# A two-block transformer kernel: the order of the first projection's columns, adaptive-weight units beside value turning, squares at the front of the sparse heads

## The reference

```python
mod = silu(c) @ w_ada + b_ada                       # six chunks: shift, scale, gate, twice
h = rms_norm(x, g_attn_pre) * (1 + scale_a) + shift_a
d_q, d_k, d_v, s_q, s_k, s_v, i_q, i_k, i_w = split(h @ w_in)      # 5456 columns
# differential attention, 8 heads: rope on q1,q2,k1,k2; (softmax(q1 k1) - lam * softmax(q2 k2)) v; rms_norm of the output
# sparse attention, 8 heads: score[t,s] = sum over 16 index heads of i_w[t,h] * relu(i_q[t,h] . i_k[s]);
#   each query keeps its 64 best keys; softmax over those; one key and one value for all heads
mixed = concat(diff_out, dsa_out) @ w_o
```

## Time and profile before

| | |
|---|---|
| three runs | 2812.94 us (median; 2812.19 to 2818.18) |
| the profiled execution | 2820.23 us, span 2818.4 us |
| mean granted TensorE clock | 0.945 of full speed |
| PE busy, share of the span | 92% |
| DVE, ACT, POOL busy | 51%, 37%, 10% |
| DMA queues | 503.83 MB, mean 179 GB/s |

### The profile page before, as it was taken

The page is one execution under the profiler, slowest core; times in us unless marked ns, Lnnn a source line. Parts: engine busy times, 40 slices in busy tenths (PEclk is TensorE's granted clock), DMA queues, the critical chain, the costliest instruction groups (busy, mean ns, idle before and its releaser), DMA issues. The chain is left out here.

```text
span 2818.4 us, 47985 instructions
## 1 busy us (share of the span) xinstructions
PE 2606.4 (92%) x19936; PEld 2404.8 (85%) x19936; DVE 1433.0 (51%) x1866; ACT 1040.0 (37%) x1322; POOL 284.3 (10%) x369
## 2 busy tenths in 40 slices
PE   5999988969999999999789979799899999999998
PEld 3888846949999999999779937358799999999998
DVE  3577756856764444344353354524455555554443
ACT  3523244334333343333243325223344444443332
POOL 4000121420000000011221000101100000000000
PEclk8999989979999999999889979779899999999999
DMA  8777866936775555555535402003455555554553
GB/s 300 260 278 271 258 215 236 330 110 237 259 272 184 181 191 179 170 188 181 156 106 170 151 15 75 15 1 120 141 172 180 181 186 181 179 179 165 179 190 108
DMA packets 263852, 503.83 MB, mean 179 GB/s; under 512 B 17168, under 2 KB 26299, under 8 KB 263483
## 3 DMA queue, kind: packets, MB, share of 16 engines
q1 hardware_dynamic: 249888, 492.99, 52.2%
q10 hardware_dynamic: 13867, 9.50, 1.3%
HBM read 498.05 MB, written 2.10 MB: 177 GB/s over the span
## 5 line engine op out<-in xcount | busy, mean ns | idle before, releaser
L1220 DVE TENSOR_TENSOR w_lo<-raw,w_hi 128x2048 fp32r<-128x2048 f32 (+2 forms) x386 | 862.1, 2233 | 1019.9 <-ACT w_hi L776 1019.3
L1788 PE MATMUL bank<-x_hi,w_hi 128*128 128x256 f32 (+3 forms) x4608 | 1314.1, 285 | 51.6 <-DVE w_lo L1220 18.8
L1789 PE MATMUL bank<-x_lo,w_hi 128*128 128x256 f32 (+3 forms) x4608 | 1311.0, 284 | 0.0
L1790 PE MATMUL bank<-x_hi,w_lo 128*128 128x256 f32 (+3 forms) x4608 | 1309.0, 284 | 0.0
L776 ACT ACTIVATE w_hi<-raw 128x2048 fp32r<-128x2048 f32 (+2 forms) x386 | 719.4, 1864 | 1070.2 <-PE bank L1790 919.1
L1788 PEld LDWEIGHTS bank<-x_hi,w_hi 128*128 128x128 f32 (+1 forms) x4608 | 876.9, 190 | 77.7 <-DVE w_lo L1220 38.6
L1790 PEld LDWEIGHTS bank<-x_hi,w_lo 128*128 128x128 f32 (+1 forms) x4608 | 877.9, 191 | 0.0
L1789 PEld LDWEIGHTS bank<-x_lo,w_hi 128*128 128x128 f32 (+1 forms) x4608 | 873.7, 190 | 0.2 <-issue 0.2
L1788 PE MATMUL bank<-hid_hi,w_hi 128*128 128x256 f32 x1408 | 400.6, 285 | 7.9 <-POOL hid_lo L662 6.6
L1789 PE MATMUL bank<-hid_lo,w_hi 128*128 128x256 f32 x1408 | 399.9, 284 | 0.0
L1790 PE MATMUL bank<-hid_hi,w_lo 128*128 128x256 f32 x1408 | 399.8, 284 | 0.0
(11 more groups left out here) (279 smaller groups left out, 1545.3 us busy)
## 6 DMA issues: line engine op xcount, KB each, us to landing
raw<-in_w_ada SPq DMA_DIRECT2D x88, 1024.0 KB, 6.0
raw<-in_w_gate SPq DMA_DIRECT2D x88, 1024.0 KB, 5.2
raw<-in_w_up SPq DMA_DIRECT2D x88, 1024.0 KB, 5.2
raw<-in_w_in SPq DMA_DIRECT2D x68, 1024.0 KB, 5.7
raw<-in_w_down SPq DMA_DIRECT2D x64, 1024.0 KB, 5.0
raw<-in_w_down SPq DMA_DIRECT2D x32, 768.0 KB, 4.3
raw<-in_w_o SPq DMA_DIRECT2D x16, 1024.0 KB, 6.9
raw<-in_w_out SPq DMA_DIRECT2D x16, 1024.0 KB, 5.1
```

What stands on the lines that cost most here:

```text
L1220: dve.tensor_tensor(w_lo[ps][:, 0:width], raw[slot][:, 0:width], w_hi[ps][:, 0:width], ALU.subtract).then_inc(raw_free[slot], 1)
L1788: pe.matmul(out, wh[:, k, c], hi(k0 + k), start=a0, stop=False)
L1789: pe.matmul(out, wh[:, k, c], lo(k0 + k), start=False, stop=False)
L1790: ins = pe.matmul(out, wl_[:, k, c], hi(k0 + k), start=False, stop=z)
```

## The change

Four things.

1. The projection's columns come in another order: differential queries and keys before sparse queries. Rotation 2 is now that of the differential queries, 3 that of the differential keys, 4 that of the sparse queries; gathers, scatters and POOL's wait counts follow.
2. The four units of w_ada block `ADA_INDEX` stand between the value turnings, those of the next block beside index heads 4 to 7. The last rotation (r = 4) stands after index head 5 on PE and after index head 6 on DVE.
3. ACT puts all eight pieces of rotation 3 back before the ReLU of index head 0, and the four of rotation 4 after index heads 8 to 11. PE waits for the return of rotations 2 and 3 before head 0, and for that of rotation 4 before head 8; ACT waits for it at g = 3, before it overwrites the gathering tile.
4. ACT's squares for the differential heads stand at the front of each step of the sparse heads.

```diff
-ORDER_IN1 = [10, 8, 9, 6, 7, 0, 1, 2, 3, 4, 5]
+ORDER_IN1 = [10, 8, 9, 0, 1, 2, 3, 6, 7, 4, 5]
...
-            (rows_iq[:, :, :], 0, RA), (rows_sq[:, :, :], 2, RB), (rows_d[:, 0:2, :], 0, RA), (rows_d[:, 2:4, :], 0, RA))]
+            (rows_iq[:, :, :], 0, RA), (rows_d[:, 0:2, :], 0, RA), (rows_d[:, 2:4, :], 0, RA), (rows_sq[:, :, :], 2, RB))]
...
                 elif n == 6:
-                    gather(2, 32, T_SQ, rows_sq)
+                    gather(2, 16, T_DQ, rows_d[:, 0:2, :])
...
                 elif n == 8:
-                    gather(3, 16, T_DQ, rows_d[:, 0:2, :])
+                    gather(3, 16, T_DK, rows_d[:, 2:4, :])
...
                 elif n == 10:
-                    scatter(2, 32, T_SQ, rows_sq)
-                    gather(4, 16, T_DK, rows_d[:, 2:4, :])
+                    scatter(2, 16, T_DQ, rows_d[:, 0:2, :])
+                    gather(4, 32, T_SQ, rows_sq)
...
+            scatter(3, 16, T_DK, rows_d[:, 2:4, :])
+            take_row(ADA_INDEX)
             for h in range(16):
...
-                if h in (3, 11):
-                    take_row(ADA_INDEX + h // 8)
-                elif h in (7, 15):
+                if h in (3, 12):
                     take_columns(ADA_INDEX + h // 8)
-                if h < 8:
-                    scatter(3, 16, T_DQ, rows_d[:, 0:2, :], h)
-                else:
-                    scatter(4, 16, T_DK, rows_d[:, 2:4, :], h - 8)
+                elif h == 8:
+                    take_row(ADA_INDEX + 1)
+                if 8 <= h < 12:
+                    scatter(4, 32, T_SQ, rows_sq, h - 8)
...
                 for g in range(g0, g1):
+                    if kind(g) == "dsa":
+                        act.wait_ge(h_taken, g - 7)
+                        squares("diff", part=g - 8)
...
+                        if g == 3:
+                            act.wait_ge(rows_back[4], 16 * 4)
                         take_out(g - 1)
-                    if kind(g) == "dsa":
-                        act.wait_ge(h_taken, g - 7)
-                        squares("diff", part=g - 8)
...
+            ada_quarter(ADA_INDEX, 0)
             pe.wait_ge(bank_freed, BLOCKS_IN1 * 4 + 4)
-            turn_values(0, [proj[:, T_DV + h, :] for h in range(8)] + [proj[:, T_SV, :]], False)
-            rotate_rows(4)
+            turn_values(0, [proj[:, T_DV + h, :] for h in range(8)] + [proj[:, T_SV, :]], False,
+                        lambda j: ada_quarter(ADA_INDEX, j // 3 + 1) if j % 3 == 1 else None)
...
-                if h % 8 < 4:
-                    ada_quarter(ADA_INDEX + h // 8, h % 8)
-                elif h % 8 == 7:
-                    ada_columns(ADA_INDEX + h // 8)
+                if h == 2:
+                    ada_columns(ADA_INDEX)
+                elif 4 <= h < 8:
+                    ada_quarter(ADA_INDEX + 1, h - 4)
+                elif h == 10:
+                    ada_columns(ADA_INDEX + 1)
+                if h == 5:
+                    rotate_rows(4)
...
+                if g == 8:
+                    pe.wait_ge(rows_back[4], 16 * 4)
...
-            pe.wait_ge(rows_back[2], 16 * 4)
-            for r in (3, 4):
+            for r in (2, 3):
                 pe.wait_ge(rows_back[r], 16 * 8)
```

More of the change, by code:

```diff
@@ L706, in _ @@
             for r, (src, sin, cos, _, _, _) in enumerate(turns1):
-                pool.wait_ge(rows_in[r], 16 * (2, 8, 4, 8, 8)[r])
+                pool.wait_ge(rows_in[r], 16 * (2, 8, 8, 8, 4)[r])
                 if r >= 2:
@@ L1451, in _ @@
             take_values(0, 9, 2, lambda j: vtok[:, :, j, :])
-            add_rows(4)
             dve.wait_ge(iw_turned, 1)
@@ L1469, in _ @@
                 ins.then_inc(i_added, 1)
+                if h == 6:
+                    add_rows(4)
             dve.wait_ge(i_added, 16)
@@ L1977, in rotate, with turn_values @@
                     ins.then_inc(r_sum, 1)
-            def turn_values(first, tiles, meta):
+            def turn_values(first, tiles, meta, beside=None):
                 for j, src in enumerate(tiles):
@@ L1989, in turn_values @@
                     ins.then_inc(v_turned, 1)
+                    if beside is not None:
+                        beside(j)
+            ada_quarter(ADA_INDEX, 0)
             pe.wait_ge(bank_freed, BLOCKS_IN1 * 4 + 4)
-            turn_values(0, [proj[:, T_DV + h, :] for h in range(8)] + [proj[:, T_SV, :]], False)
-            rotate_rows(4)
+            turn_values(0, [proj[:, T_DV + h, :] for h in range(8)] + [proj[:, T_SV, :]], False,
+                        lambda j: ada_quarter(ADA_INDEX, j // 3 + 1) if j % 3 == 1 else None)
             pe.wait_ge(r_out, 4)
```

## The result

The changed kernel takes 2802.44 us (median of 20 runs, 2795.9 to 2815.53). The kernel before takes 2816.95 us in the same comparison (20 runs, 2806.73 to 2832.08). The ratio is 0.9947, with a 95% interval of 0.9933 to 0.9961: about 14.9 us faster, between 11 and 19, where 18.7 were forecast.

What follows compares the result with a forecast made beforehand. PE, 92% busy, bounds the kernel; gains come where it idles or runs at low clock. 17.0 + 1.7 - 0 = 18.7 us off gives 2794.2 us (from a 2812.94 median); range 2788 to 2806, forecast's own 2790 to 2799.

Steps and rivals of the forecast that it cites:

- The return of the rows: Ahead of head 0: differential rows, last issued at about 351.7, are back at 358.5, 11 us early; the 7.33 us wait goes.
- The start of the index heads: Behind the value turnings: index head 0 can start near 351.6 (before 352.22), the first ReLU near 352.4 (before 353.90).
- Four units ride along for nothing: Value turnings: four w_ada units fit between them at no cost, index head 0 still starting near 351.6, before 352.22.
- The loop of index heads: Index head 0 to head 0: PE bound first, then DVE, clock up; head 0 at about 369.6, 17.0 us earlier.
- tight for none: Units beside index heads 4 to 7: loads done by 359, needed at 355, 357, 359 and 361, so none late.
- Its own sign of being wrong: Wrong if the loop's clock reads 0.50, ACT holds the first ReLU past 355, or the heads exceed 73 us.
- Head 0's ramp: Start of the attention heads, 386.6 to 398.9 at clock 0.70: carried over unchanged, with some 2 us possible gain.
- the clock falls in the second half of the loop: Rival: index heads 8 to 15, without units between them, lose the clock; 6 us less gained, 2800 us; chance 0.14.
- low from the value turnings on: Rival: clock low from the turnings through the index loop; 3.6 us slower than before, 2816.5; chance 0.06.
- Squares: Sparse heads: PE's waits for a square at g = 11 and 15 go, 1.7 us; bounds 0 and 1.7.
- Projection: Projection, n6: four more gathers delay the next w_hi by 1.3 us; costed at nothing, up to 1 us if PE is ahead.
- The sum: Whole kernel: 17.0 us from the earlier head 0 plus 1.7 from squares, minus 0, gives 18.7 us.

Runs made afterwards that it cites:

- r3: Kernel before plus only the moved w_ada units (between turnings and beside index heads 4 to 7), old order otherwise; 2811.04 us, ratio 0.9972.
- r7: r2 with the last rotation and its adds put back behind the value turnings, ahead of index head 0; 2805.63 us, ratio 0.9956.
- r4: Kernel before plus only the squares moved to the front of the sparse heads' steps; one execution, 2814.35 us.
- r2: The change without its part on the units, which stand beside index heads 0 to 3 and 8 to 11 again; 2797.45 us, ratio 0.9944.
- r8: The change with ACT's copy of the first columns behind ReLU 1 in place of ReLU 3; 2796.15 us, ratio 0.9933.
- r6: The change with index heads in pairs, second-row units behind heads 5, 7, 9 and 11, first columns copied behind ReLU 1; 2792.05 us, ratio 0.9910.
- r1: The changed kernel measured once more, nothing edited, against the kernel before; 2806.28 us, ratio 0.9948.
- r9: r6 with the second row's four units and columns moved from the index loop to the start of the attention heads; 2793.37 us, ratio 0.9913.
- r5: r2 with index heads in pairs and the units regrouped behind the pairs; 2793.4 us, ratio 0.9920.

## Why the prediction was right, and where it was not

**The return of the rows: right.** The wait of 7.33 us is gone, head 0 starts on a ReLU, and nothing else took its place. r3, with the old order, still has head 0 waiting. By the times this step carries the change: r7 has the rows back early and the units and the last rotation where they were, and keeps a ratio of 0.9956. What the wait costs depends on the clock, which the sum did not ask: in the two executions whose clock was low through the loop, early rows bring head 0 from 48.93 (r4) to 45.91 us (r7), 3.0 us only. How the rest divides between rows and clock is not shown.

**The start of the index heads: right but for 0.8 us.** I put index head 0 at 351.6, 8.3 us behind the rotation; it came 9.13 us behind. The first ReLU was to come 9.1 us behind the rotation and came at 10.1, since ACT's 20 issues took 13.5 us, between my two ends. "Four units ride along for nothing" holds against the kernel before, but not against what the new order makes possible: without them the stretch is 5.96 us (r2). Before, the rotation's wait was in it; I did not ask what the turnings would take once that was gone.

**The loop of index heads: this step failed, by 4 to 5 us.** I had 18.0 us from index head 0 to head 0; it took 23.0 and 22.4. The sum counted PE's work up to head 7 "with the clock up" and left out that the first unit of the second row waits for ACT's copy behind ReLU 3. I had moved the first ReLU and not what stood behind it. The wait is 0.6 to 0.9 us, and the clock that fell with it made the next 7 us half as fast. With the copy two ReLUs earlier the loop takes 19.1 us (r8). About half of the last 1.1 us is another wait that the prediction had excluded: "tight for none" was said of the units' transfers, and in r8 and r6 the fourth unit is 0.53 us late.

**Its own sign of being wrong.** The prediction said that it is wrong if the clock reads 0.50 in the loop. It reads 0.53 from 357.7 to 364.6, and head 0 starts at 376.4 and not near 370. So the time came out in the range while the account of the loop did not.

**Head 0's ramp: right.** Carried over unchanged, from head 0's scores to the first turning it was 7.3 us and is 7.2.

**The clock.** The rival "the clock falls in the second half of the loop" named the price roughly (6 us; measured 3.3 to 3.9 against r8) but the wrong half. A fall late in the loop, as it described, shows in the profile after (granted clock 0.50 from 372 to 374), not in r1 or r8, and fully in r9; no run tested what caused it. The rival "low from the value turnings on" did not occur: the clock read 1.00 through the turnings, with units between them and, in r2, without. By the rule of the Trainium skill in "TensorE: Matmul & The Clock Gate", Part 4, that transposes do not engage the full clock, it would have been the likely case; no trace here bears that out. My reason against it was wrong too. I argued from how much idle time the units would fill; r2 leaves that idle time in and keeps the clock.

**Squares:** 1.7 forecast, 1.4 measured alone (r4) and in the change, within what executions differ by. **Projection:** costed at nothing, and right. From the unit of w_ada just ahead of the projection to the rotation it takes 292.85 us before, 293.08 after and 292.62 in r1_same.

**The sum.** Forecast 17.0 + 1.7 = 18.7. In the profile 11.2 + 1.4 = 12.6, in r1_same 13.3; over the runs 14.9 [11, 19]. The right mechanism, with the term of the loop some 5 us too large. The medians gain a little more than the profiles; that is within the interval, and against r4's execution of the old code the change wins 16.8 us ahead of head 0, so the profile before was one of the better ones there.

In absolute time 2794.2 us was forecast and 2802.44 measured. That is outside the forecast's own 2790 to 2799, which had a chance of 0.70, and in the upper end, which had been kept for the rivals: close to the first one's 2800, by a fall of the clock in the other half of the loop. That the range held is in part luck. Of the 8.2 us, 4.0 are that the kernel before has a median of 2816.95 in this comparison and not 2812.94, which is no merit or fault of the sum; the other 4.2 are the smaller gain.

**The version to keep** is r6_pairs: 2792.05 us, ratio to before 0.9910 against the change's 0.9947 and 0.9948. The intervals, measured in different comparisons, just touch (0.9930 and 0.9929). The loop, 15.5 us against 22.4 and 23.0, shows where it comes from: 3.3 to 3.9 us from the early copy, 3.6 from the pairs. By the times, only both together stand apart from the change.

## What to carry to other kernels

When a step moves earlier, move its followers in the same sum: the copy that frees the bank for the next writer was the term that I missed, and it was 0.17 us long. Where the clock is in play, cost a short wait by what runs behind it at half speed, not by its own length. And compare a filler with the stretch as it would be after the other edits, not as it was before: the units between the turnings looked free and only traded places with the loop.

## What the runs showed of the hardware

Index heads that contract over 64 rows run beside each other when an even and an odd one stand next to each other: 0.86 us from the start of two to the start of the unit behind them (r6), 0.85 for one alone between units (r2). A unit behind each head hides that; the four heads in 1.61 us of the earlier trace rows, where none has a unit behind it, had it in them already.

The granted clock is not told by the length of the last pause. It fell to 0.50 behind pauses of 0.63 (r1), 0.89 (after), 1.22 (before), 1.43 (r7) and 2.49 us (r5), and in r9 behind a row of lone index heads with no pause over 0.34 us. It stayed at 1.00 behind 0.68 us in r2's turnings, and behind 2.43 us in r3. In front of head 0 the same changed order waited 2.15 us in r1 and kept the clock, and 2.14 us in r8 and lost it. What decides stays open.
